# Two pairs of gate/up groups per feed-forward stage: seven block products instead of eight

## The reference

```python
def swiglu_ffn(h, w_gate, w_up, w_down):
    return (jax.nn.silu(h @ w_gate) * (h @ w_up)) @ w_down

def second_block(x, ...):
    for layer in range(DEPTH):            # DEPTH = 2
        h = rmsnorm(x, norm_mix_g[layer])
        ...                               # layer 0: Fourier and convolution heads; layer 1: pooling
        x = x + y
        h = rmsnorm(x, norm_ffn_g[layer])
        x = x + swiglu_ffn(h, ffn_w_gate[layer], ffn_w_up[layer], ffn_w_down[layer])
    return rmsnorm(x, final_g)
```

## Time and profile before

| | us |
|---|---|
| device time, median of 3 runs | 724.7 (724.29 to 725.46) |
| the profiled execution's own time | 724.69 |
| its span, first to last instruction | 722.9 |
| TensorE busy | 709.7 (98% of the span) |
| VectorE busy | 498.4 (69%) |
| ScalarE busy | 397.1 (55%) |
| first feed-forward stage, about | 330 to 515 |
| second feed-forward stage, about | 531 to 717 |

### The profile page before, as it was taken

The page is one execution under the profiler, slowest core; times in us unless marked ns, Lnnn a source line. Parts: engine busy times, 40 slices in busy tenths (PEclk is TensorE's granted clock), DMA queues, the critical chain, the costliest instruction groups (busy, mean ns, idle before and its releaser), DMA issues.

```text
span 722.9 us, 9536 instructions
## 1 busy us (share of the span) xinstructions
PE 709.7 (98%) x3812; PEld 617.6 (85%) x3812; DVE 498.4 (69%) x799; ACT 397.1 (55%) x616; POOL 12.6 (2%) x18
## 2 busy tenths in 40 slices
PE   6999999999999999999999999999999999999996
PEld 5888889989999999888888888888888888888885
DVE  5789999798977889976754545545776455454544
ACT  3156536965775778778634444344755433444323
POOL 0000000000310001000000000000000000000000
PEclk8999999999999999999999999999999999999999
DMA  8999997599836359434755454555236554555101
GB/s 329 418 421 413 422 403 262 172 392 349 342 118 233 118 175 263 145 117 174 289 178 181 189 205 181 175 178 194 95 123 234 200 200 174 178 195 206 63 1 58
DMA packets 23469, 158.40 MB, mean 219 GB/s; under 512 B 2625, under 2 KB 2881, under 8 KB 5249
## 3 DMA queue, kind: packets, MB, share of 16 engines
q1 hardware_dynamic: 22464, 152.82, 56.4%
q0 software_dynamic: 960, 4.98, 2.5%
HBM read 156.74 MB, written 1.05 MB: 218 GB/s over the span
## 4 chain that ended last, share of the span: by engine, by line
PE 84%; DVE 9%; ACT 5%; DMA 1%; issue 1%; SPq 0%; DVEq 0%
PE pb L1640 21%; PE pb L1642 21%; PE pb L1641 21%; PE pb L1712 14%; DVE raw L1071 3%; DVE w L1068 3%; PE pb L1959 2%; PE pb L2064 1%; PE pb L2132 1%; ACT w L665 1%; PE pb L1987 1%; DMA x<-x_dram 1%; ACT t L783 1%; ACT r L780 1%; DVE r L1068 1%
## 5 line engine op out<-in xcount | busy, mean ns | idle before, releaser
L1068 DVE TENSOR_TENSOR w<-raw,w 128x2048 fp32r<-128x2048 f32 x95 | 216.9, 2290 | 142.8 <-ACT w L665 142.7
L665 ACT ACTIVATE w<-raw 128x2048 fp32r<-128x2048 f32 x99 | 188.5, 1913 | 144.6 <-PE pb L1642 114.7
L1640 PE MATMUL pb<-w,r 128*128 128x512 f32 (+1 forms) x608 | 238.8, 393 | 0.2 <-DVE r L1068 0.2
L1642 PE MATMUL pb<-w,r 128*128 128x512 f32 (+1 forms) x608 | 235.5, 387 | 0.0
L1641 PE MATMUL pb<-w,r 128*128 128x512 f32 (+1 forms) x608 | 235.0, 387 | 0.0
L1642 PEld LDWEIGHTS pb<-w,r 128*128 128x128 f32 x608 | 114.1, 188 | 23.8
L1640 PEld LDWEIGHTS pb<-w,r 128*128 128x128 f32 x608 | 114.2, 188 | 22.9 <-DVE r L1068 0.6
L1641 PEld LDWEIGHTS pb<-w,r 128*128 128x128 f32 x608 | 114.3, 188 | 22.3
L1640 PE MATMUL pb<-r,w 128*128 128x256 f32 x288 | 82.5, 287 | 0.3 <-DVE r L1068 0.3
L1642 PE MATMUL pb<-r,w 128*128 128x256 f32 x288 | 81.5, 283 | 0.0
L1641 PE MATMUL pb<-r,w 128*128 128x256 f32 x288 | 81.5, 283 | 0.0
(11 more groups left out here) (215 smaller groups left out, 668.3 us busy)
## 6 DMA issues: line engine op xcount, KB each, us to landing
raw<-w_dram SPq DMA_DIRECT2D x129, 1024.0 KB, 4.9
ow<-w_dram SPq DMA_DIRECT2D x8, 1024.0 KB, 16.2
ow<-w_dram SPq DMA_DIRECT2D x8, 512.0 KB, 17.2
oh<-w_dram SPq DMA_DIRECT2D x2, 1024.0 KB, 22.1
w<-w_dram POOLq DMA_DIRECT2D x2, 1024.0 KB, 14.3
x<-x_dram SPq DMA_DIRECT2D x2, 512.0 KB, 5.7
f<-rc_dram POOLq DMA_DIRECT2D x1, 1024.0 KB, 5.1
acc<-row_dram POOLq DMA_DIRECT2D x2, 512.0 KB, 4.7
```

The lines of the kernel that those rows point to most:

```text
L665: return e.activation(out, in_, ACT.Copy, **kw)
L1068: return e.tensor_tensor(out, a, b, op)
L1640: e.matmul(out, a_hi, b_hi, start=start, stop=False)
L1642: return e.matmul(out, a_lo, b_hi, start=False, stop=stop)
```

## The change

In each feed-forward stage groups 3 and 4 are done together, and groups 7 and 8 (`PAIRS = (3, 7)`). The activations of the stage are seen as four blocks: two halves of tokens by two halves of rows (four `kt` each). The weights of the two groups are four slabs: two halves of rows by two groups. Eight block products of 12 passes each stood here before (2 x 48 = 96 passes). Now there are seven (`SEVEN`), by a Strassen-Winograd scheme, so 84 passes.

- Three slabs enter as they are (`11`, `21`, `22`) and four as sums of slabs (`e`, `g`, `f`, `h`). DVE makes the sums in `form_sums`: four per pair, each 128 x 2048, in the tile `chain` (that is `F2`) or in a raw tile. The slab `11` is loaded into `chain` rather than into the ring; the other three raw slabs stay in the ring until their last use. Each of the seven operands is a slab of its own for ACT's high part and DVE's low part, where there were four.
- Four of the products take sums of activation blocks. Per stage DVE makes them once: `block_sums`, eight instructions of 128 x 512 behind `hidden(0)`; `block_high` is four ACT copies behind group 1's `fill(k)`; `block_low` is four DVE subtractions of 128 x 512 behind group 1's `fill(k)`. They live in `F3` and in `MX`, which lies over `F0` and `F1`.
- Each product has one PSUM bank. ACT copies the first to SBUF (`snap`), DVE makes the four results with seven instructions of 128 x 512 (`made_from`).
- In a pair the order on TensorE is 11, 21, e, turn, g, down, f, 22, down, h. The group after the pair turns both groups of the pair between its two halves. Gates, hidden tiles and splits are placed anew in the queues.
- POOL's load of `rc` goes behind the two row loads and waits until the last `h` slab of layer 0 is split, since `F2` is in use until then.

```diff
+PAIRS = (3, 7)
+SEVEN = ("11", "21", "e", "g", "f", "22", "h")
...
+            plan.append(("11", None, layer, 0, i))
+            plan.append(("part", None, layer, 0, i + 1))
+            plan.append(("21", None, layer, 4, i))
+            plan.append(("part", None, layer, 4, i + 1))
+            plan.extend(("form", name, layer, i) for name in ("e", "g"))
+            plan.append(("down", "ffn_w_down_2", layer, i - 2))
+            plan.extend(("form", name, layer, i) for name in ("f", "22"))
+            plan.append(("down", "ffn_w_down_2", layer, i - 1))
+            plan.append(("form", "h", layer, i))
...
 (POOL)
-            e.dma_start(rc, rcnt_d).then_inc(s_rc, 16)
             e.dma_start(prow[:, :], row_d[0]).then_inc(s_prow, 16)
             e.wait_ge(s_cv3, 1)
             e.dma_start(frow[:, :], row_d[1]).then_inc(s_frow, 16)
+            e.wait_ge(s_lo, LOW_AT[AT["h", 0, PAIRS[-1]]])
+            e.dma_start(rc, rcnt_d).then_inc(s_rc, 16)
...
 (ACT)
+            def block_high(layer):
+                for n, made in ((0, 5), (2, 6), (1, 7), (3, 8)):
+                    p.wait_ge(s_blk, 8 * layer + made)
+                    copy(mixes(n, 0), blocks[:, (1, 0, 2, 3)[n], :, :]).then_inc(s_bhi, 1)
...
+                    if kind == "two":
+                        k = AT["11", layer, i]
+                        fill(k)
...
+                        snap(layer, i)
+                        fill(k + 1)
+                        fill(k + 2)
+                        gates(layer, i, [0])
+                        hidden_high(layer, i - 1)
+                        fill(k + 3)
+                        fill(k + 4)
+                        fill(k + 5)
+                        gates(layer, i + 1, [1])
+                        fill(k + 6)
+                        gates(layer, i + 1, [0])
+                        fill(k + 7)
+                        fill(k + 8)
+                        gates(layer, i, [1])
+                        continue
                     k = AT["gu", layer, i]
                     fill(k)
+                    if i == 1:
+                        block_high(layer)
...
 (DVE)
+            def form_sums(k, kind, name, layer, *at_):
+                g = at_[-1]
+                if kind == "11":
...
+                    tt_(chain, chain, raw_of(top)[:, :], ADD).then_inc(s_form, 1)
+                elif name == "e":
...
+                    tt_(chain, chain, raw_of(low_)[:, :], ADD).then_inc(s_form, 1)
+                    p.wait_ge(*form_made("e", layer, g))
+                    tt_(raw_of(top)[:, :], raw_of(top)[:, :], raw_of(low_)[:, :], ADD).then_inc(s_form, 1)
+                elif name == "22":
...
+                    tt_(chain, chain, raw_of(own_)[:, :], ADD).then_inc(s_form, 1)
...
+                    if kind == "two":
+                        k = AT["11", layer, i]
+                        fill(k)
+                        fill(k + 1)
+                        made_from(layer, i, "c11")
+                        fill(k + 2)
+                        hidden(layer, i, [0])
+                        hidden_low(layer, i - 1)
+                        fill(k + 3)
+                        made_from(layer, i, "u2", "c11")
+                        fill(k + 4)
+                        made_from(layer, i, "t", "u2")
+                        fill(k + 5)
+                        made_from(layer, i, "u3", "t")
+                        made_from(layer, i, "c22", "t")
+                        fill(k + 6)
+                        hidden(layer, i + 1, [1])
+                        made_from(layer, i, "c12", "c22")
+                        fill(k + 7)
+                        hidden(layer, i + 1, [0])
+                        fill(k + 8)
+                        made_from(layer, i, "c21", "u3")
+                        hidden(layer, i, [1])
+                        continue
                     k = AT["gu", layer, i]
                     fill(k)
+                    if i == 1:
+                        block_low(layer)
...
                     fill(k + 1)
                     hidden(layer, i)
+                    if i == 0:
+                        block_sums(layer)
...
 (PE)
+            def two_groups(layer, i):
+                for name in ("11", "21", "e"):
+                    seven(layer, i, name)
+                turn_hidden(layer, i - 1)
+                seven(layer, i, "g")
+                for c in range(2):
+                    down(layer, i - 2, c, range(2))
+                for name in ("f", "22"):
+                    seven(layer, i, name)
+                for c in range(2):
+                    down(layer, i - 1, c, range(2))
+                seven(layer, i, "h")
...
+                    if len(hts) == 2:
+                        gate_up(layer, i, range(0, 4), range(2))
+                        for j in hts:
+                            turn_hidden(layer, j)
+                        gate_up(layer, i, range(4, 8), range(2))
```

More of the change, by code:

```diff
@@ L12 @@
 NG = FF // 256
-STEPS = [step for i in range(NG) for step in [("gu", i)] + ([("d", i - 2)] if i >= 2 else [])]
-STEPS += [("d", NG - 2), ("d", NG - 1)]
+PAIRS = (3, 7)
+UNITS_OF = [("two" if i in PAIRS else "one", i) for i in range(NG) if i - 1 not in PAIRS]
+SEVEN = ("11", "21", "e", "g", "f", "22", "h")
+SUMS = ("c11", "u2", "t", "u3", "c22", "c12", "c21")
 RT = 8
@@ L99 @@
 OWN = [i for i, p in enumerate(PLAN) if p[0] in ("u", "g", "y") or p[0] == "heads" and p[1] != "pool_map_2"]
-RING = [i for i in range(len(PLAN)) if i not in OWN]
-MATS = [i for i in RING if PLAN[i][0] not in ("first", "mod")]
+RING = [i for i in range(len(PLAN)) if i not in OWN and PLAN[i][0] not in ("11", "form")]
+MATS = [i for i in range(len(PLAN)) if i not in OWN and PLAN[i][0] not in ("first", "mod", "part")]
 MODS = [i for i in RING if PLAN[i][0] == "mod"]
@@ L117, in slab_of, with pair_at, part, turned_in @@
 def slab_of():
-    at, k = {}, 30
-    for layer in range(2):
-        if layer:
-            at["pool"] = k
[L123 to L127, removed]
+    at = {}
+    for k, i in enumerate(MATS):
+        kind, name, *where = PLAN[i]
+        if kind == "gu" and where[1] == 0:
+            at["gu", where[0], where[2]] = k
+        elif kind == "down":
+            at["d", where[0], where[1]] = k
+        elif kind in ("11", "21"):
+            at[kind, where[0], where[2]] = k
+        elif kind == "form":
+            at[name, where[0], where[1]] = k
+        elif (kind, name) == ("heads", "pool_map_2"):
+            at["pool"] = k
     return at
 AT = slab_of()
+def pair_at(layer, i):
+    return len(PAIRS) * layer + PAIRS.index(i)
+def part(layer, k0, i):
+    return PLAN.index(("part", None, layer, k0, i + 1))
+def turned_in(kind, i):
+    if kind == "two":
+        return [i - 1]
+    return [i - 2, i - 1] if i - 2 in PAIRS else [i - 1] if i else []
+def halves_made():
+    at = {}
+    for layer in range(2):
+        for kind, i in UNITS_OF:
+            for j, a in ((i, 0), (i, 1)) if kind == "one" else ((i, 0), (i + 1, 1), (i + 1, 0), (i, 1)):
+                at[layer, j, a] = len(at) + 1
+    return at
+HALVES = halves_made()
+GROUP_OF = {n: x[0:2] for x, n in HALVES.items()}
 class Outputs:
@@ L313, in outputs @@
     return o
+FIRST_RING = (4, 5, 6, 7)
 OUT = outputs()
@@ L574, in freed @@
                 return s_hid, hid_at(*at)
+            if kind == "seven":
+                if at[2] == "11":
+                    return s_snap, pair_at(i, at[1]) + 1
+                last = {"21": "c11", "g": "u2", "e": "t", "f": "c22", "22": "c12", "h": "c21"}[at[2]]
+                return s_fork, fork_at(i, at[1], last)
             if kind == "ht":
@@ L612, in _ @@
                 else:
[L613 to L616, removed]
+                    emptied.append(emptied_at(i))
+                    if i == MATS[5]:
                         e.dma_start(cst[:, P:NC], cst_d[:, P:NC]).then_inc(s_cst, 16)
@@ new lines, in block_low, with made_from @@
+            def block_low(layer):
+                for m, n in enumerate((0, 2, 1, 3)):
+                    p.wait_ge(s_bhi, 4 * layer + m + 1)
+                    tt_(mixes(n, 1), blocks[:, (1, 0, 2, 3)[n], :, :][:, :, :], mixes(n, 0).bitcast(f32),
+                        SUB).then_inc(s_blo, 1)
+            def made_from(layer, i, name, *others):
+                product_, at_, x, y, op = {
+                    "c11": ("21", 1, None, 0, ADD), "u2": ("g", 0, None, 0, ADD), "t": ("e", 2, None, 0, SUB),
+                    "u3": ("f", 0, None, 0, ADD), "c22": ("f", 3, 2, None, SUB), "c12": ("22", 2, None, 2, ADD),
+                    "c21": ("h", 0, None, 0, ADD)}[name]
+                p.wait_ge(*ended("seven", layer, i, product_))
+                p.wait_ge(s_snap, pair_at(layer, i) + 1)
+                for other in others:
+                    p.wait_ge(s_fork, fork_at(layer, i, other))
+                x, y = (bank_of("seven", layer, i, product_)[:, :] if z is None else snaps[:, z, :] for z in (x, y))
```

(1 more changed line is left out.)

225 lines of the change are left out of this document (181 added, 44 removed).

## The result

The changed kernel takes **736.0 us** (median of 4 runs, 735.2 to 738.0); the kernel before takes 724.5 on the same chip. The ratio is 1.0163 with a 95% interval of 1.0138 to 1.0188. So the change makes the kernel 1.6% slower. The forecast was 734.8 with a range of 729 to 743, slower.

What follows compares the result with a forecast made beforehand. The prediction took TensorE, busy 98% of the span, as the bound. Saved passes -10.9, stage-start stalls +6.1 and +3.8, pair turns +8.0 and clock +3.1 gave +10.1 us, so 734.8 us, range 729 to 743.

Steps and rivals of the forecast that it cites:

- The gain: Feed-forward pairs on TensorE: one block product of 12 passes, 2.73 us, saved in each of four pairs, 10.9 us.
- Prices on DVE: Added DVE steps: split or slab sum 2.20 us start to start, 512-wide instruction 0.61, or 0.73 when waited for.
- Edit one: Stage starts: block steps queued before hidden(1) stall TensorE in group 2 by 6.1 us in layer 0, 3.8 in layer 1.
- Edit two: Turns behind the pairs: TensorE waits 2.0 us for the last hidden tile, four times, 8.0 us, from two ACT waits.
- Edits at no cost: Loads of raw tiles, rc and the next pair's 11: covered, no cost; at most 5 us if rc's cover were gone.
- The clock: TensorE's clock falls to half once, after layer 0's stall: 3.1 us lost, bounds 0 and 6.2.
- The sum: Whole kernel: -10.9 + 6.1 + 3.8 + 8.0 + 3.1 = +10.1 us on 724.69, giving 734.8 us.
- No fall of the clock: Rival: same stalls but no half clock after layer 0's stall, 731.7 us; chance 25%.
- Every step at its full record: Rival: DVE and ACT steps cost whole record and signal; pair stalls 4.1, starts 7.0 and 4.7, 745.0 us; chance 12%.
- Pairs covered: Rival: DVE and ACT keep pace in pairs, only stage starts stall; 723.7 us, 726.8 with the clock's fall; chance 7%.
- spare time counts: Rival: DVE's idle time and three slabs of lead absorb the added work, all stalls vanish, 713.8 us; chance 4%.

Runs made afterwards that it cites:

- both moves: Changed kernel with ScalarE's pair high parts ahead of the waiting silus and DVE's block sums, hidden(1), high copies and low subtractions re-placed: 714.15 us, ratio 0.9855.
- the block steps alone: Kernel before plus only each stage's eight block sums, four high copies and four low subtractions, read by nothing: 737.4 us, ratio 1.0182.
- the two moved lines: Changed kernel with two lines moved in ScalarE's queue, so high parts in a pair precede the silus waiting for c22 and c12: 726.9 us, ratio 1.0030.
- the block steps moved: Changed kernel with block sums before the stage's first fill, hidden(1) before slab 36's split, high copies and low subtractions in group 2: 725.6 us, ratio 1.0008.
- the filler: Changed kernel with unneeded TensorE products (20 passes in layer 0, 12 in layer 1) before group 2's wait for the bank: 733.1 us, ratio 1.0119.
- the sums alone: Kernel before plus only the eight block sums of each stage, without high copies or subtractions: 731.6 us, ratio 1.0086.

## Why the prediction was right, and where it was off

- *The gain, 10.9 us.* Right: 48 passes fewer, and the kernel with both moves gets 10.6 of it.
- *Prices on DVE.* Right. Sums of blocks took 2.49 for four, and 2.86 for the four of which three wait; the queue was free for the split of slab 35 at 351.65, walked as 352.1 with a stage that began 0.4 later. A slab sum, which the trace of before did not have, takes 2.28 to 2.29 at full record, bounded at 2.2 to 2.3.
- *Edit one.* 6.1 and 3.8 forecast, 6.0 and 3.7 measured; shown by the block steps alone, which give the same waits, and by their move, which takes them away.
- *Edit two.* 2.0 forecast four times, 2.0 measured four times. The two waits for ScalarE were forecast at 2.4 and are 2.38. That they are the cause was argued then and is shown by the two moved lines.
- *Edits at no cost.* `rc`, the raw tiles and the pairs' own banks made no wait of TensorE in any traced run.
- *The clock.* This is the term that was mis-sized: one fall of 3.1 us forecast, three falls of 6.7 in the profiled execution. Layer 0's start cost 2.4 rather than 3.1. The step that failed is the comparison of each wait with the one idle time of the trace of before, 4.6 us: I took the 3.8 and the 2.0 as too short. Both can be followed by a fall.
- *The sum.* 734.8 against 736.0. Waits and passes alone give 731.7 as forecast and 731.3 with the measured waits; the rest of the median, 4.7 us, is by difference, the clock and what differs ahead of the stages. So the waits came 0.4 us below the forecast and the rest, forecast at 3.1, 1.6 above it.
- *Rivals.* No fall of the clock: out. Every step at its full record: out, the walk by start to start holds within 0.1 us at each wait. The rule of the Trainium skill's page "VectorE: DVE Perf Modes", section "The DRAIN you can't avoid", on the emptied pipe was weighed there; in the changed kernel too the instruction behind a split starts 2.20 us after it (356.26 to 358.46) with a record of 2.28. The prediction left out that the same section lets a next instruction that is not held start earlier, so the trace is at odds with the rule as quoted there rather than with the page. Pairs covered and spare time counts: both out as forecasts. The first (726.8 with the clock's fall) is what the moved lines on ScalarE make of the kernel, 726.9; the second (713.8) is what both moves make of it, 714.15.

## What to carry to other kernels

Work that fits into an engine's idle share still costs time if it stands in the queue ahead of an instruction that another engine waits for, all of it that the margin at that place and the engine's own idle time ahead of it don't cover: 7.6 us of block steps made TensorE wait 6.0 us in one layer and 3.7 in the other. Before adding steps look for the place where the producer's margin is smallest (0.6 us here), and walk that place from start to start. Where two engines feed each other in turn, put the independent step ahead of the one that waits: the same instructions in another order made 714 us out of 736. Price a wait of TensorE with the slow passes that may follow it.

## What the runs showed of the hardware that I had not expected

The granted clock can fall at much less idle time than the 4.6 us of the trace of before. With waits of 1.9 us, it fell behind one of four pairs in the profiled execution of the changed kernel, behind two of four with the block steps moved, and behind none of four with the filler. With 3.5 us it fell in layer 1 of the changed kernel and of the one with ScalarE's order, and in layer 0 with the sums alone, but not in layer 1 with the block steps alone. With 5.9 us it fell each time (three traces). In the stages it never fell behind waits of 1.4 us or less. Each fall made the passes behind it take 0.43 us rather than 0.227, for 3.4 to 6.1 us, which is 1.6 to 2.9 us lost.

So the same wait can cost another time in another trace. How much it varies between executions of one kernel is not shown, since each kernel was traced once. The spread of the times doesn't show it either. Kernels with such waits spread over 3 us (735.2 to 738.0, 735.9 to 739.0) and the kernel before over 1.1 in 19 executions of one series (724.2 to 725.3), but over 2.5 in 7 of the other, and the kernel with both moves, which has no such wait, over 2.2 in four. Part of the spread lies ahead of the stages: group 1's transposes start between 351.3 and 353.0 in the three rows above.
